# Gate and up of each feed-forward tile as a 2x2 block product of seven terms, with split weights, in a two-layer fp32 encoder

## The chip, the core and the metric

The kernel runs on one core of one Trainium2 chip. The metric is the device time of one execution in microseconds (us), the median of three runs. The matrix engine is TensorE (PE, with its weight loads apart as PEld), the elementwise engines are VectorE (DVE), ScalarE (ACT) and GpSimd (POOL), and SyncE (SP) issues the transfers.

## What is computed

Two sequences, 528 and 272 tokens with 16 learned ones in front of each, go through the same two layers. Together they are T = 800 tokens of 1024 channels. The part that the change touches is the feed-forward stage, which stands four times in the program (ffn1 and ffn2 of both layers):

```python
def swiglu(x, w_gate, w_up, w_down):
    return (jax.nn.silu(x @ w_gate) * (x @ w_up)) @ w_down
...
for layer in range(DEPTH):
    h = h + 0.5 * swiglu(rms_norm(h, norm_ffn1[layer]), ...)
    hn = rms_norm(h, norm_mix[layer])
    h = h + (even_mixer(hn, ...) if layer % 2 == 0 else fourier_mixer(hn, w_out_fourier[layer // 2]))
    h = h + 0.5 * swiglu(rms_norm(h, norm_ffn2[layer]), ...)
return rms_norm(h, norm_final)[:, N_META:]
```

Everything is float32. Gate and up are each 1024 x 2816 (D_FF), down is 2816 x 1024, so that D_FF makes 22 tiles of 128. The even layer's mixer is windowed attention beside a pooling mixer; the odd layer's is a Fourier transform over positions and channels with one output projection.

## The kernel before

**Layout.** Channels lie on the 128 partitions, so `h` is 8 tiles (KD) of 128 channels by 800 tokens. A matmul has a 128x128 block of weights as its stationary side and half of the tokens (392, 400, 400 and 384 columns in the four feed-forward stages, called f = 0 to 3 here) as its moving side. A stage that needs fewer tokens has them left out.

**Precision.** Each float32 operand is held as two fp32r parts, hi and lo. ScalarE makes hi (a copy with rounding), VectorE makes lo (the operand less hi). A product then takes three matmuls: hi by hi, hi weights by lo tokens, lo weights by hi tokens. For the weights, `split_hi` (L463) and `split_lo` (L678) do this for a whole block of 1024 or 1408 columns, out of `raw`, two slots that SyncE fills with one transfer a block (L235).

**A feed-forward stage.** `ffn` on each engine runs two halves of 11 tiles. In a half, a hardware loop takes the tiles: block 0 is the gate, block 1 the up weights of the tile, each 8 k tiles x 3 matmuls x 2 token halves = 48 matmuls, into two banks each. So a tile of D_FF takes 96 matmuls. VectorE takes the banks out times `rstd`, the reciprocal norm (L768 gate, L773 up), ScalarE takes Silu (L518), VectorE multiplies (L777), ScalarE and VectorE split the product into `act_hi` and `act_lo` (L522, L781). After the 11 tiles a second loop does down: 8 output tiles m, each 11 x 6 = 66 matmuls, and VectorE adds the result to `h` (L807, or L818 by token pieces).

**The norm.** While down of the second half runs, each finished channel tile of `h` is squared (L504), summed over tiles (L720), and, scaled by the gain, split to `xn_hi` (L495) and `xn_lo` (L709). The next stage's matmuls can begin on these before the norm is known. TensorE does `statistics` (L1048) after the first block and `broadcast` (L1058) in the middle of the second, with the power on GpSimd (L355) between them. Before f = 1 and f = 3 the split waits until the projection is done (`LATE_NORMS`).

**Order.** Each engine's instructions stand in the order written. Engines wait for one another by counting semaphores. The weights of block n+2 are split while block n's results are taken out: there are two slots, and so TensorE has at most one block in hand. In the Fourier stage, `fold` on GpSimd (L424, L425) adds and subtracts two halves of the raw block before the split, and the sine part of the result comes back by `odd` (L662) to be added to `h` by GpSimd (L447, L448) and VectorE.

The gate and up transfers are 512 KB, a block each.

## Time and profile before

| | |
|---|---|
| median of 3 runs | 2777.54 us (2775.79 to 2780.04) |
| span of the profiled execution | 2767.7 us |
| PE busy | 2682.6 us (97%) |
| PEld busy | 2602.0 us (94%) |
| DVE busy | 1025.1 us (37%) |
| ACT busy | 683.9 us (25%) |
| POOL busy | 97.2 us (4%) |
| weights and data read | 160.73 MB, 59 GB/s over the span |

The span runs from the first to the last instruction of the profiled execution. Its device time is not listed apart from the three runs; their median is 9.8 us over the span, and this difference is taken to stay. Busy PE counts a matmul until its result has landed, and matmuls overlap, so how fast TensorE goes is read from the spacing of their starts: a stretch of time over the number of matmuls in it.

### The profile page before, as it was taken

How to read it: one execution, taken by the hardware profiler on the slowest of the kernel's cores; microseconds unless marked ns; L12 is line 12 of the kernel's file. 1: busy time of each engine (PE TensorE's matmuls, PEld its weight loads, DVE VectorE, ACT ScalarE, POOL GpSimd, SP SyncE). 2: the span in 40 equal slices, each digit the busy share in tenths (PEclk: the TensorE clock that was granted, in tenths of full speed). 3: DMA queues.
4: the chain of work that ended last, by engine and by line, in shares of the span. 5: the costliest groups of instructions: out<-in, count | busy, mean ns of one | idle time of the engine just before them, and what ended most of it. 6: DMA issues, size and time to landing. Idle time of an engine off the chain costs nothing.

```text
span 2767.7 us, 35751 instructions
## 1 busy us (share of the span) xinstructions
PE 2682.6 (97%) x14700; PEld 2602.0 (94%) x14700; DVE 1025.1 (37%) x1312; ACT 683.9 (25%) x925; POOL 97.2 (4%) x101
## 2 busy tenths in 40 slices
PE   7999999999999999999999999999998799999997
PEld 7999999998359999999999999999998799999997
DVE  5332233333534333233334332233345633223333
ACT  4331122221542332112222221122233322112211
POOL 0000000004000000000000000000003300000000
PEclk9999999999889999999999999999999999999998
DMA  3122122212001121111211121112121222212221
GB/s 110 61 66 65 51 61 64 70 48 88 1 8 54 53 61 66 56 61 59 67 57 54 61 66 63 53 61 63 63 70 35 63 61 61 73 56 61 61 74 58
DMA packets 42096, 164.66 MB, mean 59 GB/s; under 512 B 4928, under 2 KB 5184, under 8 KB 41920
## 3 DMA queue, kind: packets, MB, share of 16 engines
q1 hardware_dynamic: 40464, 160.65, 18.3%
q10 hardware_dynamic: 1584, 3.38, 0.3%
q8 instruction: 29, 0.48, 0.1%
q14 instruction: 19, 0.16, 0.0%
HBM read 160.73 MB, written 3.28 MB: 59 GB/s over the span
## 4 chain that ended last, share of the span: by engine, by line
PE 74%; issue 21%; DVE 3%; ACT 1%; POOL 0%; DMA 0%; ACTq 0%; POOLq 0%; DVEq 0%; SPq 0%
PE banks L1016 68%; PE banks L1007 2%; PE banks L1136 1%; PE banks L1171 1%; PE banks L1150 1%; DVE sum_sq L720 0%; DVE w_lo L698 0%; ACT score L571 0%; PE banks L1048 0%; PE banks L1058 0%; DMA raw<-w_fourier_dram 0%; DVE h L995 0%; DVE xn_lo L709 0%; ACT square L504 0%; DVE score L902 0%
## 5 line engine op out<-in xcount | busy, mean ns | idle before, releaser
L1016 PE MATMUL banks<-xn_hi,w_hi 128*128 128x400 f32 (+2 forms) x3104 | 814.6, 343 | 26.1 <-DVE xn_lo L709 19.2
L1016 PE MATMUL banks<-xn_lo,w_hi 128*128 128x400 f32 (+2 forms) x3104 | 812.2, 343 | 0.0
L1016 PE MATMUL banks<-xn_hi,w_lo 128*128 128x400 f32 (+2 forms) x3104 | 811.5, 343 | 0.0
L463 ACT ACTIVATE w_hi<-raw 128x1024 fp32r<-128x1024 f32 (+1 forms) x258 | 294.4, 1141 | 1646.2 <-PE banks L1016 1645.9
L1016 PEld LDWEIGHTS banks<-xn_hi,w_hi 128*128 128x128 f32 x3104 | 571.5, 189 | 30.6 <-issue 23.6
L1016 PEld LDWEIGHTS banks<-xn_lo,w_hi 128*128 128x128 f32 x3104 | 572.4, 189 | 0.0
L1016 PEld LDWEIGHTS banks<-xn_hi,w_lo 128*128 128x128 f32 x3104 | 572.2, 188 | 0.0
L678 DVE TENSOR_TENSOR w_lo<-raw,w_hi 128x1024 fp32r<-128x1024 f32 (+1 forms) x258 | 344.5, 1335 | 71.0 <-ACT w_hi L463 70.6
L1016 PE MATMUL banks<-act_hi,w_lo 128*128 128x400 f32 (+2 forms) x1408 | 368.0, 342 | 0.0
L1016 PE MATMUL banks<-act_hi,w_hi 128*128 128x400 f32 (+2 forms) x1408 | 367.9, 343 | 0.0
L1016 PE MATMUL banks<-act_lo,w_hi 128*128 128x400 f32 (+2 forms) x1408 | 367.9, 342 | 0.0
L773 DVE TENSOR_TENSOR up_t<-banks,rstd 128x800 f32<-128x800 f32 (+2 forms) x88 | 86.1, 979 | 487.7 <-PE banks L1016 487.7
L1016 PEld LDWEIGHTS banks<-act_lo,w_hi 128*128 128x128 f32 x1408 | 259.0, 188 | 0.1
L1016 PEld LDWEIGHTS banks<-act_hi,w_hi 128*128 128x128 f32 x1408 | 258.9, 188 | 0.0
L1016 PEld LDWEIGHTS banks<-act_hi,w_lo 128*128 128x128 f32 x1408 | 258.6, 188 | 0.0
L768 DVE TENSOR_TENSOR gate_t<-banks,rstd 128x800 f32<-128x800 f32 (+2 forms) x88 | 86.2, 979 | 394.7 <-PE banks L1016 394.3
L818 DVE SCALAR_TENSOR_TENSOR h<-banks,h 128x256 f32<-128x256 f32 (+3 forms) x112 | 36.4, 384 | 240.9 <-PE banks L1016 240.9
L807 DVE SCALAR_TENSOR_TENSOR h<-banks,h 128x800 f32<-128x800 f32 x32 | 31.7, 992 | 246.7 <-PE banks L1016 246.7
L522 ACT ACTIVATE act_hi<-up_t 128x800 f32 (+5 forms) x88 | 76.1, 865 | 88.4 <-DVE up_t L777 88.4
L777 DVE TENSOR_TENSOR up_t<-up_t,gate_t 128x800 f32<-128x800 f32 (+2 forms) x88 | 86.3, 980 | 9.2
L781 DVE TENSOR_TENSOR act_lo<-up_t,act_hi 128x800 f32 (+5 forms) x88 | 86.2, 979 | 0.6
L518 ACT ACTIVATE gate_t<-gate_t 128x800 f32<-128x800 f32 (+2 forms) x88 | 74.7, 849 | 13.8 <-DVE gate_t L768 13.6
(131 smaller groups left out, 1206.4 us busy)
## 6 DMA issues: line engine op xcount, KB each, us to landing
raw<-gate_up_dram SPq DMA_DIRECT2D x176, 512.0 KB, 3.6
raw<-down_dram SPq DMA_DIRECT2D x64, 704.0 KB, 4.0
raw<-w_in_dram SPq DMA_DIRECT2D x10, 512.0 KB, 3.5
raw<-w_fourier_dram SPq DMA_DIRECT2D x8, 576.0 KB, 3.8
raw<-w_out_dram SPq DMA_DIRECT2D x8, 512.0 KB, 3.6
h<-x_dram ACTq DMA_DIRECT2D x8, 400.0 KB, 6.5
y_dram<-h SPq DMA_DIRECT2D x8, 400.0 KB, 2.5
raw<-tables_dram SPq DMA_DIRECT2D x4, 704.0 KB, 4.0
```

Of the source, the lines that this page charges most:

```text
L463: A.activation(w_hi[s][:, 0:k * P], raw[s][:, 0:k * P], ACT.Copy).then_inc(w_hi_done, 1)
L518: A.activation(gate_t[:, 0:W], gate_t[:, 0:W], ACT.Silu).then_inc(silu_done, 1)
L522: A.activation(act_hi[:, bass.ds(i * T, W)], up_t[:, 0:W], ACT.Copy)\
L678: V.tensor_tensor(w_lo[s][:, 0:k * P], raw[s][:, 0:k * P], as32(w_hi[s][:, 0:k * P]), ALU.subtract).then_inc(w_ready, 1)
L768: V.tensor_tensor(two(gate_t[:, 0:W]), slot(0, C), two(rstd[:, 0:W]), ALU.mult)\
L773: V.tensor_tensor(two(up_t[:, 0:W]), slot(1, C), two(rstd[:, 0:W]), ALU.mult)\
L777: V.tensor_tensor(up_t[:, 0:W], up_t[:, 0:W], gate_t[:, 0:W], ALU.mult)\
L781: V.tensor_tensor(act_lo[:, bass.ds(i * T, W)], up_t[:, 0:W], as32(act_hi[:, bass.ds(i * T, W)]), ALU.subtract)\
L807: return V.scalar_tensor_tensor(two(h[:, m, :]), slot(m % 2), 0.5, two(h[:, m, :]), ALU.mult, ALU.add)
L818: last = V.scalar_tensor_tensor(h[:, m, t:t + n], banks[:, 2 * (m % 2) + b, c:c + n], 0.5, h[:, m, t:t + n], ALU.mult, ALU.add)
L1007: ins = M.matmul(out, a, b, start=first and j == 0, stop=last and j == 2)
L1016: ins = M.matmul(banks[:, 2 * s + half, 0:cols], a, b[:, half * cols:(half + 1) * cols], start=first and j == 0, stop=last and j == 2)
```

## The change

**The tile product.** The two blocks of a tile, gate and up, are seen as the columns of a 2x2 matrix of blocks. Its inner index is the parity of the k tile (4 even, 4 odd), and the columns of the other factor are the two token halves. The eight block products become seven, in Winograd's form of Strassen's scheme. Each is 4 k tiles x 3 matmuls on one half of the tokens, 12 matmuls, and all 12 of a product go into one bank. So a tile takes 84 matmuls. Four of the seven left sides are sums of weight quarters: S1 = A21 + A22, S2 = S1 - A11, S4 = A12 - S2, S3 = A11 - A21, made by VectorE for each tile (`weight_sum`). The seven right sides, B11, T1, T2, B22, T3, B21 and N4, are made once a stage from `h` and the gain (`gained_tile`, `form_sum`, `form_high`, `form_low`).

**Sums in the banks.** P6, P7 and P4 go on accumulating in the bank of P1, and P3 in the bank of P5. Between them ScalarE copies the partial sum out (4 copies of half the tokens a tile, counted by `copied`), and VectorE adds and scales.

**Weights in units.** In place of two blocks there are 6 slots of 512 columns. A unit is one left side, or 2 or 3 k tiles of down. The tables at the head of the file give each unit's place; ScalarE is 4 units ahead of TensorE, VectorE 3, the sums 5. A transfer brings a whole tile, 1 MB.

**The rest.** Down runs in four chunks of 5, 5, 6 and 6 tiles in place of two of 11, so `h` is added to 32 times a stage, not 16; its matmuls are as many as before (8 x 22 x 6 = 1056 a stage). The forms alias buffers of the stage before, and before f = 1 and f = 3 (`late_forms`) they are split after the projection, four k tiles in one instruction. There are no hardware loops any more. In the Fourier stage the folded block is 3 units. The third part of the tables is split after the first 8 tiles of the transform.

```diff
+PRODUCTS = ("P1", "P5", "P6", "P3", "P7", "P2", "P4")
+WEIGHT_OF = ("A11", "S1", "S2", "S4", "S3", "A12", "A22")
+FORM_OF = ("B11", "T1", "T2", "B22", "T3", "B21", "N4")
+NS = 6
+SUM_AHEAD, HI_AHEAD, LO_AHEAD = 5, 4, 3
...
+        def form_sum(f, name, k):
+            C = FFN_COLS[f]
+            if name == "T1":
+                dve.wait_ge(gained, f * KD + 2 * k + 1)
+                ins = V.tensor_tensor(form(f, "T1", k), b12[:, 0:C], form(f, "B11", k), ALU.subtract)
...
+            ins.then_inc(form_added, 1)
...
+            if NORMS[i] in NORM_FFN:
+                f, k = NORM_FFN[NORMS[i]], m // 2
+                if m % 2 == 0:
+                    add_square(i, m)
+                    form_sum(f, "T1", k)
+                    form_low(f, "B11", k)
+                else:
+                    form_sum(f, "T2", k)
+                    form_sum(f, "T3", k)
+                    form_sum(f, "N4", k)
+                    dve.wait_ge(form_added, ADD_AT[f, "N4", k])
+                    form_low(f, "T1", k)
+                    add_square(i, m)
+                    for name in ("T2", "B22", "T3", "B21", "N4"):
+                        form_low(f, name, k)
...
+                for j in range(CHUNK_AT[c], CHUNK_AT[c] + n_tiles):
...
+                    if not first:
+                        up_first(j - 1, J - 1)
+                        dve.wait_ge(g1_done, J)
+                        dve.wait_ge(g2_done, J)
+                        V.tensor_tensor(gate[1 - j % 2][:, 0:W], gate[1 - j % 2][:, 0:W], rstd[:, 0:W],
+                                        ALU.mult).then_inc(scaled, 1)
+                    weights_to(n0)
+                    if not first:
+                        up_second(J - 1)
+                    weights_to(n0 + 1)
...
+                    if not first:
+                        product(j - 1, J - 1)
+                    weights_to(n0 + 2)
+                    if not first:
+                        act_low(j - 1, J - 1)
+                    weights_to(n0 + 3)
+
+                    dve.wait_ge(unit_done, n0 + 4)
+                    dve.wait_ge(copied, 4 * J + 3)
+                    V.tensor_tensor(g[:, C:W], banks[:, SUM53, 0:C], g[:, C:W], ALU.add).then_inc(g2_done, 1)
+                    weights_to(n0 + 4)
...
+                    dve.wait_ge(unit_done, n0 + 6)
+                    V.tensor_tensor(g[:, 0:C], banks[:, OWN2, 0:C], g[:, 0:C], ALU.add).then_inc(g1_done, 1)
...
+            def product(j, q):
+                n, J, name = GU[f][j] + q, f * FF_TILES + j, PRODUCTS[q]
+                pe.wait_ge(w_ready, n + 1)
...
+                elif name == "P3":
+                    bank = SUM53
+                    pe.wait_ge(copied, 4 * J + 2)
+                else:
+                    bank = j % 2
+                    pe.wait_ge(copied, 4 * J + {"P6": 1, "P7": 3, "P4": 4}[name])
...
+                for k in range(KP):
+                    if j == 0:
+                        pe.wait_ge(form_ready, LO_AT[f, FORM_OF[q], k])
+                    a_hi, a_lo = weights(n, k)
+                    b_hi, b_lo = xf_hi[:, at, k, 0:C], xf_lo[:, at, k, 0:C]
+                    M.matmul(out, a_hi, b_hi, start=fresh and k == 0, stop=False, skip_group_check=True)
+                    M.matmul(out, a_hi, b_lo, start=False, stop=False, skip_group_check=True)
+                    ins = M.matmul(out, a_lo, b_hi, start=False, stop=k == KP - 1, skip_group_check=True)
+                ins.then_inc(unit_done, 1)
```

Three places show what stands on an engine in a row. The first is VectorE in a tile in the middle of a stage. Before, the tile's loop body (gate and up out of the banks, two weight blocks, the product, its split):

```order
L768 TENSOR_TENSOR gate_t<-banks,rstd 128x784
L677 ISA
L678 TENSOR_TENSOR w_lo<-raw,w_hi 128x1024
L771 REGISTER_ALU
L773 TENSOR_TENSOR up_t<-banks,rstd 128x784
L777 TENSOR_TENSOR up_t<-up_t,gate_t 128x784
L677 REGISTER_ALU
L678 TENSOR_TENSOR w_lo<-raw,w_hi 128x1024
L781 ISA
L781 TENSOR_TENSOR act_lo<-up_t,act_hi 128x784
```

Now, the first 12 of the 19 instructions of a tile (`xf` are forms, `w_sum` the sums of weight quarters, `g` the gate, `p` the copy of P5's bank); seven more follow: three sums, three lo parts and an add to the gate:

```order
L1065 TENSOR_TENSOR up<-banks,rstd 128x392
L1095 TENSOR_TENSOR g<-g,rstd 128x784
L903 TENSOR_TENSOR w_lo<-w_sum,w_hi 128x512
L1069 TENSOR_TENSOR up<-up,p 128x392
L1071 TENSOR_TENSOR up<-up,rstd 128x392
L903 TENSOR_TENSOR w_lo<-w_sum,w_hi 128x512
L1077 TENSOR_TENSOR act<-up,g 128x784
L903 TENSOR_TENSOR w_lo<-raw,w_hi 128x512
L1083 TENSOR_TENSOR act_lo<-act,act_hi 128x784
L887 TENSOR_TENSOR w_sum<-raw 128x512
L903 TENSOR_TENSOR w_lo<-raw,w_hi 128x512
L1112 TENSOR_TENSOR g<-banks,g 128x392
```

Six elementwise instructions a tile have become 19, the two weight blocks seven units and four sums; the product of the tile before stands among the units of this one. The second place is VectorE at the program's start, one channel tile before:

```order
L709 SCALAR_TENSOR_TENSOR xn_lo<-h,gain,xn_hi 128x528
L709 SCALAR_TENSOR_TENSOR xn_lo<-h,gain,xn_hi 128x256
L720 TENSOR_TENSOR sum_sq<-sum_sq,square 128x800
L678 TENSOR_TENSOR w_lo<-raw,w_hi 128x1024
L709 SCALAR_TENSOR_TENSOR xn_lo<-h,gain,xn_hi 128x528
```

and now a pair of channel tiles, the second of the four pairs:

```order
L940 TENSOR_TENSOR sum_sq<-sum_sq,square 128x800
L956 TENSOR_TENSOR xf<-b,xf 128x392
L972 TENSOR_TENSOR xf_lo<-xf,xf_hi 128x392
L960 TENSOR_TENSOR xf<-xf 128x392
L962 TENSOR_TENSOR xf<-xf,b 128x392
L965 TENSOR_TENSOR xf<-xf 128x392
L972 TENSOR_TENSOR xf_lo<-xf,xf_hi 128x392
L940 TENSOR_TENSOR sum_sq<-sum_sq,square 128x800
L972 TENSOR_TENSOR xf_lo<-xf,xf_hi 128x392 x5
L893 TENSOR_TENSOR w_sum<-raw,w_sum 128x512
L903 TENSOR_TENSOR w_lo<-w_sum,w_hi 128x512
```

A pair takes eleven instructions of half the tokens where two tiles took four. The third place is ScalarE in the Fourier output projection, one output tile before:

```order
L662 ACTIVATE odd<-banks 128x404
L486 ACTIVATE w_hi<-w_fold 128x1024
L487 ACTIVATE w_hi<-raw 128x128
L504 ACTIVATE square<-h 128x800
L662 ACTIVATE odd<-banks 128x404
```

and now:

```order
L863 ACTIVATE odd<-banks 128x404
L566 ACTIVATE w_hi<-w_sum 128x512
L566 ACTIVATE w_hi<-raw 128x128
L566 ACTIVATE w_hi<-w_sum 128x512
L596 ACTIVATE square<-h 128x800
L615 ACTIVATE xf<-h,gain 128x384
L615 ACTIVATE xf<-h,gain 128x128
L615 ACTIVATE xf<-h,gain 128x256
L863 ACTIVATE odd<-banks 128x404
```

Three pieces of the gained tile now stand before the next `odd`, which were done after the last tile before. The hi parts here belong to output tile m+2, and GpSimd folds that block after it has added `odd` of tile m, where before it folded it ahead of that.

## Rows read from the trace of the kernel before

**Rows 1.** The page: busy us, share of the span and instructions of each engine.
```profile
PE 2682.6 (97%) x14700; PEld 2602.0 (94%) x14700; DVE 1025.1 (37%) x1312; ACT 683.9 (25%) x925; POOL 97.2 (4%) x101
```

**Rows 2.** Stretches: us, busy of PE, PEld, DVE, ACT, POOL, clock, DMA share, GB/s.
```profile
35.00:600.00 565.00, 565.00 (x3144) 564.88 (x3144) 198.33 (x229) 140.46 (x137) 0.27 (x3) 1.00 0.19 61
...
914.00:1483.00 569.00, 568.46 (x3118) 568.43 (x3119) 193.97 (x179) 141.19 (x138) 0.00 (x0) 1.00 0.19 61
...
1495.00:2050.00 555.00, 555.00 (x3055) 555.00 (x3054) 189.06 (x174) 112.89 (x115) 0.00 (x0) 1.00 0.19 63
...
2115.00:2180.00 65.00, 44.66 (x216) 42.21 (x216) 48.20 (x73) 21.82 (x34) 34.50 (x29) 0.94 0.26 79
...
2200.00:2747.00 547.00, 542.96 (x3105) 542.32 (x3103) 183.53 (x202) 107.73 (x110) 0.00 (x0) 1.00 0.19 60
```

**Rows 3.** The order in time, TensorE: start, us (L1007 puts three matmuls a step into one bank).
```profile
2073.11 0.28 PE L1007 MATMUL banks<-dft_hi,xn_lo 128*106 128x258 f32 x1
...
2074.91 0.28 PE L1007 MATMUL banks<-dft_hi,xn_lo 128*92 128x258 f32 x1
...
2173.74 0.35 PE L1007 MATMUL banks<-xn_lo,w_hi 128*128 128x404 f32 x1
...
2175.05 0.34 PE L1007 MATMUL banks<-xn_hi,w_lo 128*128 128x404 f32 x1
```

**Rows 4.** Queues in the straight-line stretch 2068 to 2115: packets, MB, share.
```profile
q8 instruction: 3, 0.05, 0.4%
```

**Rows 5.** Groups by shape: engine, operation, count | busy us, mean ns | idle before.
```profile
L678 DVE TENSOR_TENSOR w_lo<-raw,w_hi 128x1024 fp32r<-128x1024 f32 x194 | 240.7, 1241 | 56.1 <-ACT w_hi L463 55.8
...
L463 ACT ACTIVATE w_hi<-raw 128x1024 fp32r<-128x1024 f32 x194 | 205.9, 1061 | 1085.3 <-PE banks L1016 1085.0
...
L777 DVE TENSOR_TENSOR up_t<-up_t,gate_t 128x800 f32<-128x800 f32 x44 | 43.7, 993 | 4.6
...
L955 DVE TENSOR_TENSOR xn_lo<-banks,xn_hi 128x404 fp32r<-128x404 f32 x8 | 4.6, 579 | 18.6 <-ACT xn_hi L647 18.6
...
L662 ACT ACTIVATE odd<-banks 128x404 f32<-128x404 f32 x8 | 4.1, 507 | 19.1 <-PE banks L1007 19.1
```

**Rows 6.** The order in time of VectorE and ScalarE behind an up block.
```profile
1003.34 0.99 DVE L773 TENSOR_TENSOR up_t<-banks,rstd 128x800 f32<-128x800 f32 x1 [4.92 <-PE banks L1016]
...
1004.43 0.99 DVE L777 TENSOR_TENSOR up_t<-up_t,gate_t 128x800 f32<-128x800 f32 x1
...
1005.34 1.22 DVE L678 TENSOR_TENSOR w_lo<-raw,w_hi 128x1024 fp32r<-128x1024 f32 x1
...
1005.55 0.87 ACT L522 ACTIVATE act_hi<-up_t 128x800 f32 x1 [1.07 <-DVE up_t L777]
...
1006.58 0.99 DVE L781 TENSOR_TENSOR act_lo<-up_t,act_hi 128x800 f32 x1
```

**Rows 7.** The chain that ended last, around the four stage starts: start, us.
```profile
35.21 565.31 PE banks L1016 x3144
...
883.94 1.00 DVE h L931
...
890.52 11.11 PE banks L1016 x48
...
914.54 5.63 PE banks L1016 x21
...
2059.01 3.97 DMA raw<-tables_dram
...
2170.14 5.26 PE banks L1007 x27
```

**Rows 8.** GpSimd's groups in the Fourier output projection, by shape.
```profile
L425 POOL TENSOR_TENSOR w_fold<-raw 128x512 f32<-128x512 f32 x8 | 13.1, 1631 | 0.0
...
L424 POOL TENSOR_TENSOR w_fold<-raw 128x512 f32<-128x512 f32 x8 | 11.5, 1440 | 26.0 <-DMA raw<-w_fourier_dram 16.1 <-PE banks L1007 9.9
...
L447 POOL TENSOR_TENSOR h<-h,odd 128x265 f32<-128x265 f32 x8 | 8.3, 1034 | 12.0 <-ACT odd L662 12.0
```

More of the change, by code:

```diff
@@ L99, in k_tiles @@
[L99 to L111 removed]
+CHUNKS = (5, 5, 6, 6)
+CHUNK_AT = (0, 5, 10, 16)
@@ new lines, in gained_tile @@
+        def gained_tile(f, m):
+            i, k = NORMS.index(("ffn1_0", "ffn2_0", "ffn1_1", "ffn2_1")[f]), m // 2
+            if m % 2 == 0 and k:
+                act.wait_ge(form_added, ADD_AT[f, "T3", k - 1])
+            for half, c, t, n in token_parts(f):
+                if m % 2:
+                    out = xf32[:, FORM_AT["B22" if half else "B21"], k, c:c + n]
+                elif half:
+                    out = b12[:, c:c + n]
+                else:
+                    out = xf32[:, FORM_AT["B11"], k, c:c + n]
+                last = A.activation(out, h[:, m, t:t + n], ACT.Copy,
+                                    scale=gain[:, i * KD + m:i * KD + m + 1])
+            last.then_inc(gained, 1)
```

1157 lines of the change are left out of this document (708 added, 449 removed).

## The prediction

> **What bounds the kernel now.** I read the page first. TensorE is busy 2682.6 us of 2767.7, VectorE 37%, ScalarE 25% [rows 1]. A busy share does not say what a matmul costs, so the busy time by stretch comes next, for the four feed-forward stages: 565.0 us hold 3144 matmuls, 569.0 hold 3118, 555.0 hold 3055 and 547.0 hold 3105, TensorE never waits over about 4 us in any of them, and its clock is 1.00 of full, the 2.4 GHz level [rows 2]. A matmul starts every 565.0/3144 = 0.1797 us at 392 columns, 555.0/3055 = 0.1817 at 400, and 543.0/3105 = 0.1749 at 384. These stages are 2236 us of the span. The reader is to see that a matmul saved there is 0.18 us saved, as long as nothing else becomes late, and that VectorE works there only 198 of 565 us. Last I read the chain of waits at the starts of the stages, where TensorE does wait.
>
> **What is taken away.** A tile has 84 matmuls for 96: 12 x 22 = 264 fewer a stage. That is 264 x (0.1797 + 0.1817 + 0.1817 + 0.1749) = 189.6 us. Down keeps its matmuls.
>
> The Trainium skill, TensorE: Matmul & The Clock Gate, section "Wait — 56ns, not 53.3ns?", gives the spacing of back-to-back matmuls as the columns over 2.4 GHz and about 2.5 ns, so 169 ns at 400 columns. The trace disagrees: 181.7. By the page the 1056 matmuls would be worth some 176 us, by the rows 189.6.
>
> **What a matmul costs in the new form.** Twelve matmuls in a row now go into one bank; before, two banks took turns. The nearest rows are L1007, which does just this. At 258 columns 15 spacings take 1.80 us, 120 ns, 12.5 over 258/2.4; at 404 columns 7 take 1.31, 187 ns, 18.8 over 404/2.4 [rows 3]. The old form at 400 has 15.0 over. So the bounds are -2.5 and +3.8 ns, over 7392 product matmuls -18 to +28 us. Both rows are near zero on either side; I take +5 us, the side of the row nearer in columns.
>
> **VectorE in a tile.** This is where the change could fail. Times for 512 and 400 columns lie between rows: 0.579 us for 404, 0.993 for 800, 1.241 for 1024 [rows 5] give 0.575 and 0.69. A tile has 11 instructions of 512 (7 lo parts, 4 sums), 7.6 us; 5 of 400, 2.9; 3 of 800, 3.0: 13.5 us. Instructions that do not depend on the last one start 0.08 early (1004.43 + 0.99 against 1005.34 [rows 6]), which takes back about 1. TensorE needs 84 x 0.1817 = 15.3. So VectorE goes from some 35% to 80 to 90%, but it still fits. ScalarE has 7 of 512 (0.60 each, between 0.507 and 1.061 [rows 5]), 4 copies of 400 (0.51) and two of 800 (0.87 [rows 6]): 8.0 us, fits.
>
> Order can still cost. I laid a tile out, with product starts at 0, 2.2, 4.4, 6.5, 8.7, 10.9, 13.1. VectorE begins at 0.15 with the last product of the tile before, and has scaled, split units 3, 4 and 5 and made the activation by 5.8. Then it waits for the hi part of that, which ScalarE does only after its third copy: P6 ends at 6.5, copy to 7.1, hi to 8.0, lo to 9.1. The rest, 4 sums, 4 lo parts and 2 adds, is 6.6 us and ends at 15.0 to 15.7, when the next tile begins at 15.3. Unit 6 is ready at 10.4 and needed at 13.1; the copies are ready 0.6 us after a product and are needed 2.2 after, which leaves 1.6 us. The idle 2.3 us before the hi part is the buffer. TensorE does not wait: 0 us for the tile. Were VectorE's work to grow by over 15%, this cover would be gone.
>
> **Chunk ends.** Down of the last tile needs its activation: up out of the bank 0.6, product 1.0, hi 0.9, lo 1.0, with hand-overs 3.9 us by the same row as 1003.34 to 1007.57 with half as much to take out [rows 6]. TensorE meanwhile does 4 of 5 tiles of the first output, 24 x 0.18 = 4.3 us. It is covered by 0.4 us in the two short chunks of a stage, by 1.5 in the long ones. I take 1 us over eight places (0 to 4).
>
> **Starts of stages.** *f = 0:* before, TensorE had both blocks of tile 0 done at 35.2 + 24 x 0.18 = 39.5 [rows 7]. Now VectorE makes, for each pair of channel tiles, 11 instructions of 392 (0.48 each back to back), two sums of squares (0.9) and two weight steps (0.6): 8.5 us a pair, 7.6 for the first. It starts at about 10.5 and has the last forms at 43. P1 waits for its fourth k tile until 37, P5 until 39, P3 until 43, the broadcast of the norm until 48; tile 0 is done at 53.5. Without the change of order it would be 39.5 - 2.2. So +16 us (10 to 25; before, the same work was two instructions a tile). *f = 1:* last matmul of the projection at 883.9, next tile began at 914.5, 30.6 later [rows 7]. Now: h 1.0, square 0.9, sums and N4 5, B11 1.8, so P1 starts 8.5 us after, at the 1.2 GHz level for a few us (I count 10 matmuls at 0.33); forms of 1600 columns follow at 1.8 to 1.9 us and the norm's chain ends at 26; tile 1 starts at 30.0. Against 28.4: +1.5. *f = 2:* the forms are made beside down; VectorE needs about 11 to 12 us a pair beside 13.1 of TensorE, and with ScalarE's answers 13.8, so it is 1 to 2 us late at the end, and then T1 and the norm come late: +3.5 (0 to 8). *f = 3:* below.
>
> **Fourier stage.** The third part of the tables stood before the first evacuation and waited 3.97 us for its transfer [rows 7]; now it stands behind 8 tiles: -2. The first unit is 512 columns in place of 1152: -2. In the projection TensorE is busy 44.7 of 65 us [rows 2], 5.3 an output tile [rows 7]. ScalarE now has a loop: odd 0.5, GpSimd's two adds 1.8, the fold of the block two ahead 1.4 + 1.6 [rows 8], the hi part 0.6, the square 0.9, the gained pieces 1.3, which is 8.3 against some 7.7 now; +5 over eight. Then the late forms: the next tile starts some 2 us later than the old order would give. Together +7 (0 to 15).
>
> **The sum.** -189.6 + 5 + 0 + 1 + 16 + 1.5 + 3.5 - 2 - 2 + 7 = -159.6 us. From the profiled span of 2767.7 this is 2608. The 9.8 us between span and median stay: 2777.5 - 160 = **2618 us**.
>
> **Instruction stream.** The loops are gone, and TensorE's matmuls and weight loads all stand in line. The stretch 2068 to 2115 stands in line too, at 366 matmuls in 47 us, with three fetches [rows 4] and no wait for them; it goes faster than the products will. So 0. The Trainium skill, Runtime: NRT & Kernel Launch, section "Instruction fetch mechanics", says that a taken branch out of the window stalls and straight code streams. By it the loops would have cost something and dropping them gain; the trace shows no such stall in the loops [rows 2], and the sum would be the same.
>
> **The rivals.** *VectorE becomes the bound of the tile* (0.12). For it: 13.5 us of 15.3 and five hand-overs between VectorE and ScalarE in each tile. Against: the 2.3 us buffer. If its instructions and hand-overs come to 16.1 us a tile, TensorE waits 0.8 a tile: 88 x 0.8 = 70, 2688 us. *One bank, many waits* (0.08): each product has one or two waits of its own, and twelve matmuls into one bank cost 3.8 ns more each, 28 us in place of 5; with 20 ns at each of 616 units, 12 us more: 2653. *The forms hide* (0.05): the starts cost 5 and not 28: 2595. *Slower than before* (0.03): ScalarE's copy between P1 and P6, P5 and P3, P6 and P7, P7 and P4 is the place. It has 1.6 us of slack each. If ScalarE is held up there by the weight sums it waits for, so that each of the four copies comes 2.1 us late, 0.5 us are lost four times a tile: 176 us, over the 160 gained; 2794. It decides from a lateness of 2.05 us a copy on. *It doesn't do what it says:* the order of the built program has 7392 product matmuls; none. A chance of 0.01 lies in a gain eaten to zero by two of these at once.
>
> **How the numbers follow.** The forecast, TensorE undisturbed in the tiles, has 0.71: 2618, from 2600 to 2650 by the bounds above. The range takes in the second and third rival and part of the first: 2594 to 2665. A change under 0.2% (5.6 us) can't be told from none. Faster: 0.71 + 0.12 + 0.08 + 0.05 = 0.96; same 0.01; slower 0.03.
>
> **What would show it.** 13644 matmuls, 1056 fewer than [rows 1]. In a stretch of tiles: spacing 0.180 to 0.186 us at 400 columns, VectorE busy 80 to 90%, TensorE without waits over 0.3 us. Tile 0 of the first stage done near 53 us. The projection of the Fourier stage 67 to 72 us. If TensorE waits inside tiles for `w_lo` of VectorE, the laid-out tile is wrong; if it waits for a copy, ScalarE's order is; if the spacing is over 0.19 without waits, it is the bank.

## The result

| | before | after |
|---|---|---|
| median, us (lowest to highest, runs) | 2776.66 (2771.79 to 2780.04, 4) | 2607.76 (2607.15 to 2614.92, 4) |
| profiled execution: span, us | 2767.7 | 2605.3 |
| matmuls | 14700 | 13644 |

The ratio is 0.9406, with a 95% interval from 0.9388 to 0.9424: 169 us faster. The prediction had 2618, from 2594 to 2665. A second set of five executions of the same kernel, on the chip of experiments e8, e9 and e11, had a median of 2608.96 (2606.87 to 2610.30), ratio 0.940.

The page of after, beside [rows 1]; then the queue that brings the instructions:

```profile
PE 2496.2 (96%) x13644; PEld 2415.1 (93%) x13644; DVE 1657.6 (64%) x2900; ACT 1046.5 (40%) x2015; POOL 90.9 (3%) x101
...
q8 instruction: 110, 1.80, 0.3%
```

TensorE has 186 us less of busy time; VectorE has 633 us more and still a third of the span to spare. The straight code asks for 110 instruction packets, and TensorE has no wait for them inside a tile.

The four stretches of tiles, with the columns of [rows 2]: us, then busy time and instructions of PE, PEld, DVE, ACT, POOL.

```profile
58.00:560.00 502.00, 502.00 (x2818) 502.00 (x2817) 335.17 (x607) 200.87 (x358) 0.00 (x0) 1.00 0.20 68
881.00:1393.00 512.00, 512.00 (x2817) 512.00 (x2817) 339.76 (x541) 209.65 (x382) 0.00 (x0) 1.00 0.19 66
1420.00:1932.00 512.00, 512.00 (x2817) 512.00 (x2817) 329.58 (x512) 199.15 (x354) 0.00 (x0) 1.00 0.19 65
2087.00:2582.00 495.00, 495.00 (x2820) 495.00 (x2819) 321.04 (x566) 190.31 (x346) 0.00 (x0) 1.00 0.19 64
```

TensorE is busy for the whole of all four. A matmul starts every 502/2818 = 0.1781 us at 392 columns, 0.1818 at 400 and 0.1755 at 384. [rows 2] had 0.1797, 0.1817 and 0.1749. So twelve in a row into one bank cost nothing, within 2 ns either way. Differences of this size are not the bank's alone: in experiment e2 below, whose matmuls are the same, the pace was 174.4 ns in place of 176.1 at 384 columns, and the four stretches took 2017.1 us for 2022.8. Why is open.

One tile of after, 15.3 us, first as a stretch and then as VectorE's and ScalarE's order in time (start, us):

```profile
1003.60:1018.90 15.30, 15.30 (x86) 15.30 (x85) 12.10 (x20) 7.51 (x13) 0.00 (x0) 1.00 0.20 70
```
```profile
1003.41 0.57 DVE L1069 TENSOR_TENSOR up<-up,p 128x400 f32<-128x400 f32 x1
...
1005.11 0.98 DVE L1077 TENSOR_TENSOR act<-up,g 128x800 f32<-128x800 f32 x1
1006.01 0.69 DVE L903 TENSOR_TENSOR w_lo<-raw,w_hi 128x512 fp32r<-128x512 f32 x1
1009.28 0.99 DVE L1083 TENSOR_TENSOR act_lo<-act,act_hi 128x800 fp32r<-128x800 f32 x1 [2.58 <-ACT act_hi L698]
...
1007.98 0.50 ACT L695 ACTIVATE g<-banks 128x400 f32<-128x400 f32 x1 [1.17 <-PE banks L1440]
1008.38 0.86 ACT L698 ACTIVATE act_hi<-act 128x800 fp32r<-128x800 f32 x1
```

The tile goes as it was laid out by hand. VectorE is busy 12.1 of 15.3 us, 79%. Its one long wait, 2.58 us where the prediction had 2.3, is for the hi part of the activation, which ScalarE makes only after the copy at 1007.98.

**Where 162 us of span went.** I compared the start times of the same matmuls in both traces: the first of a stage, the first of its tile 1, the last of down (and of w_out, the output projection of the attention mixer). The prediction's terms are put on the same cuts. A start there has lost the 12 matmuls of tile 0, 2.1 to 2.2 us, which stand against its cost.

| piece of the span | before, us | after, us | difference | predicted |
|---|---|---|---|---|
| f = 0: start to tile 1 | 39.37 | 57.90 | +18.5 | +13.8 |
| tile 1 to the last matmul, four stages | 2207.4 | 2022.8 | -184.7 | -175.2 |
| f = 0's last to w_out's last (attention inside) | 292.09 | 287.75 | -4.3 | 0 |
| w_out's last to tile 1 of f = 1 | 30.98 | 33.04 | +2.1 | -0.7 |
| f = 1's last to tile 1 of f = 2 | 20.38 | 26.64 | +6.3 | +1.3 |
| f = 2's last to tile 1 of f = 3 (Fourier stage) | 153.97 | 154.27 | +0.3 | +0.9 |
| the end | 23.44 | 22.97 | -0.5 | 0 |
| sum | | | -162.3 | -159.9 |

Whether the 4.3 us of the third row belong to the change is open. The experiments, whose code is the same there, took from 287.6 to 296.5 us for it, which is more than the difference, and of the kernel before there is one trace.

### The profile page after: what moved, and what is told of

It is laid out like the page before. It is cut to its first block, busy times and chain, and to the rows that moved or that the text cites. A ratio compares the mean times of both kernels' runs of the same rounds, so it can differ in the third digit from the quotient of the medians.

```text
span 2605.3 us, 35440 instructions
## 1 busy us (share of the span) xinstructions
PE 2496.2 (96%) x13644; PEld 2415.1 (93%) x13644; DVE 1657.6 (64%) x2900; ACT 1046.5 (40%) x2015; POOL 90.9 (3%) x101
## 4 chain that ended last, share of the span: by engine, by line
PE 71%; issue 22%; DVE 4%; ACT 2%; POOL 1%; DMA 0%; POOLq 0%; ACTq 0%; DVEq 0%
PE banks L1361 26%; PE banks L1438 13%; PE banks L1440 13%; PE banks L1439 13%; PE banks L1491 2%; PE banks L1526 1%; PE banks L1505 1%; PE banks L1354 1%; DVE xf_lo L972 1%; ACT xf L615 0%; DVE xf_lo L985 0%; POOL w_sum L516 0%; POOL w_sum L518 0%; PE banks L1400 0%; ACT xf_hi L626 0%
## 5 line engine op out<-in xcount | busy, mean ns | idle before, releaser
L1438 PE MATMUL banks<-xf_hi,w_hi 128*128 128x400 f32 (+2 forms) x2464 | 848.7, 344 | 70.3 <-DVE xf_lo L985 23.4
L1439 PE MATMUL banks<-xf_lo,w_hi 128*128 128x400 f32 (+2 forms) x2464 | 848.7, 344 | 0.0
L1440 PE MATMUL banks<-xf_hi,w_lo 128*128 128x400 f32 (+2 forms) x2464 | 846.1, 343 | 0.0
L1438 PEld LDWEIGHTS banks<-xf_hi,w_hi 128*128 128x128 f32 x2464 | 466.3, 189 | 73.6 <-issue 51.7
L1440 PEld LDWEIGHTS banks<-xf_hi,w_lo 128*128 128x128 f32 x2464 | 468.5, 190 | 0.0
L1439 PEld LDWEIGHTS banks<-xf_lo,w_hi 128*128 128x128 f32 x2464 | 466.7, 189 | 0.4
L566 ACT ACTIVATE w_hi<-raw 128x512 fp32r<-128x512 f32 (+3 forms) x564 | 310.4, 559 | 373.5 <-PE banks L1361 365.6
L566 ACT ACTIVATE w_hi<-w_sum 128x512 fp32r<-128x512 f32 x368 | 230.3, 630 | 332.7 <-DVE w_sum L895 128.6
L903 DVE TENSOR_TENSOR w_lo<-raw,w_hi 128x512 fp32r<-128x512 f32 (+3 forms) x564 | 337.0, 611 | 19.3 <-ACT w_hi L566 19.3
L903 DVE TENSOR_TENSOR w_lo<-w_sum,w_hi 128x512 fp32r<-128x512 f32 x368 | 252.4, 689 | 2.6 <-ACT w_hi L566 2.6
L679 ACT ACTIVATE g<-banks 128x400 f32<-128x400 f32 (+2 forms) x88 | 43.9, 499 | 217.5 <-PE banks L1440 217.5
```

What stands on the lines that cost most here:

```text
L566: A.activation(w_hi[:, n % NS, 0:u.cols], source, ACT.Copy).then_inc(w_hi_done, 1)
L903: V.tensor_tensor(w_lo[:, n % NS, 0:u.cols], source, as32(w_hi[:, n % NS, 0:u.cols]), ALU.subtract).then_inc(w_ready, 1)
L1438: M.matmul(out, a_hi, b_hi, start=fresh and k == 0, stop=False, skip_group_check=True)
L1439: M.matmul(out, a_hi, b_lo, start=False, stop=False, skip_group_check=True)
L1440: ins = M.matmul(out, a_lo, b_hi, start=False, stop=k == KP - 1, skip_group_check=True)
```

## The experiments

Line numbers in the rows of an experiment are those of its own kernel. Unless another is named, times are set against 2607.8 us, the changed kernel.

**Is it the number of matmuls?** P2 is done twice:

```diff
-                for k in range(KP):
+                for k in [*range(KP), *range(KP)] if name == "P2" else range(KP):
```

> The twelve matmuls of P2 are done twice in each tile (the second start of the bank throws the first twelve away), so a tile has 96 matmuls again, as before the change, but in the new form: same output, 14700 matmuls. Theory (the number of matmuls sets the time of the tiles, everything else is covered): 264 more a stage at the spacings of the changed kernel, 0.178 + 0.182 + 0.182 + 0.176 us, is +189 us, so 2797 us, some 20 us over the kernel before, which is then what the starts of the stages cost. Rival A (part of the gain comes from something else, the code without loops or a faster pace in one bank): then the 96 matmuls cost clearly less than +189, and the time is at or under the 2777 of the kernel before. Rival B (VectorE or ScalarE already holds TensorE back a little in each tile): a longer tile gives that time back, so again less than +189, by the part that was waiting.

Measured: 2798.57 us (2797.09 to 2804.51), ratio to before 1.0098, interval 1.0073 to 1.0122. That is 190.8 more than the changed kernel, where 189 was expected. Both kinds of rival fall: at most a few us of the gain can belong to the straight code, and no engine was holding TensorE back in the tiles. With the same 14700 matmuls the new form is 28 us slower than the old one on the same chip (2770.35). By the cuts of the table, the starts of the stages cost 35 us in this run, the tiles and down 3.6 less than before (2203.9 for 2207.4), and the third row 4.1 less. So the price lies at the starts, not in the tiles.

**How much cover has VectorE?** Four additional instructions, eight in the second kernel, each waiting for the last (the wait and its semaphore are left out here), stand ahead of the lo part of the activation:

```diff
                     weights_to(n0 + 2)
+                    if j:
+                        for _ in range(4):
+                            V.tensor_tensor(fill[:, :], rstd[:, 0:400], rstd[:, 360:760], ALU.add)
                     if not first:
                         act_low(j - 1, J - 1)
```

> The changed kernel with four extra VectorE instructions of 400 columns in tiles 1 to 21 of each stage, each waiting for the last one (some 0.60 us each, 2.4 us in all), put just ahead of the lo part of the activation, where VectorE waits 2.6 us for ScalarE. Theory (cover of 2.3 to 2.6 us at that place): no change, within 0.2%: 2608 +- 5. Rival (VectorE is in fact the bound of the tile, or its steps are so tight that any delay passes through): 84 x 2.4 = +202 us, 2810; in between, whatever part of the 2.4 passes through times 84.

> The same with eight extra VectorE instructions, 4.8 us a tile. VectorE is idle 3.2 us in a tile of 15.3, so 1.6 us a tile are too much. Theory (cover of 3.2 us a tile, then VectorE is the bound): each chunk of five or six tiles falls behind by 1.6 a tile, of which some 2.7 us are taken by the weights that lie ready (unit 6 is ready at 10.4 and needed at 13.1) and VectorE catches up in down: 84 x 1.6 = 134 less 16 x 2.7 = 43, so +90 us, 2700 (from 2650 to 2745). Rival (much more cover than the order laid out by hand says, because TensorE is fed far ahead): under +30 us. Rival (VectorE the bound from the first addition on): +400 us.

Measured: 2603.12 us (2601.51 to 2604.26) with four, 2690.96 (2686.99 to 2694.51) with eight. Two stretches of the first, and what TensorE waited for in the second (us in total, times, longest):

```profile
881.00:1393.00 512.00, 512.00 (x2822) 511.88 (x2821) 386.52 (x626) 210.33 (x383) 0.00 (x0) 1.00 0.19 66
...
1000.00:1060.00 60.00, 60.00 (x332) 59.98 (x331) 55.18 (x89) 28.38 (x51) 0.00 (x0) 1.00 0.14 50
```
```profile
PE banks L1446 <- ACT up L711: 51.6, 42, 1.6
...
PE banks L1369 <- DVE act_lo L1085: 10.8, 16, 1.2
```

VectorE can be busy 55.18 of 60 us, 92%, and TensorE does not notice (that the kernel is 4.6 us faster than without the four is the pace spoken of above, and not explained). So the first 2.4 us a tile are free, and the rival that VectorE is nearly the bound falls. With 4.8 us the cover of 3.2 us a tile is used up: +83 us where +90 was expected. The wait that then ends last is of interest. It is not one for VectorE's weights but for ScalarE's copy `up`, 42 times. ScalarE goes through its list in order, and the hi part of a weight sum stands ahead of that copy; when VectorE is late with the sum, ScalarE waits for it and the copy comes late. One such place, ScalarE and then TensorE:

```profile
209.59 0.63 ACT L568 ACTIVATE w_hi<-w_sum 128x512 fp32r<-128x512 f32 x1 [4.77 <-DVE w_sum L889]
210.13 0.48 ACT L711 ACTIVATE up<-banks 128x392 f32<-128x392 f32 x1
...
210.75 0.42 PE L1446 MATMUL banks<-xf_hi,w_hi 128*128 128x392 f32 x1 [1.30 <-ACT up L711]
```

That is the mechanism of the prediction's slower rival. It exists, and it begins somewhere between 2.4 and 4.8 us of VectorE work a tile away from the kernel as it is.

**How late may a copy be?** `late(j, p)` is so many ScalarE instructions of 608 columns, 0.71 us each, behind the wait for the product and ahead of copy p: four at copy 4 in the first kernel, one at each of the four copies in the other.

```diff
+                    late(j, 4)
                     A.activation(up[:, C:W], banks[:, acc, 0:C], ACT.Copy).then_inc(copied, 1)
```

> The changed kernel with four extra ScalarE instructions of 608 columns (about 0.70 us each, 2.8 us in all) in tiles 1 to 21 of each stage, behind the wait for P7 and ahead of the copy that frees P7's bank for P4. The copy is ready 0.5 us after P7 ends and P4 begins 2.2 after, so the prediction has 1.65 us of slack there. Theory: 2.8 - 1.65 = 1.15 us of wait a tile at P4, 84 x 1.15 = +97 us, 2705; the hi parts behind it come 2.8 later too and may add up to 0.5 a tile: 2690 to 2750. Rival (another wait hides it, the copies have more slack than 1.65 us): under +40 us. Rival (late hi parts pass fully through VectorE to the weights): 84 x 2.8 = +235 us.

> One extra ScalarE instruction of 608 columns (0.71 us) ahead of each of the four copies out of the banks in tiles 1 to 21, so that every copy is 0.7 us late. The run with 2.85 us at the last copy alone lost 1.57 a tile, so the slack there is 1.3 us. Theory (each copy has its own 1.3 us and a lateness under it costs nothing): the tiles as they were, span 2605 +- 5. Rival (the four add up along the chain through VectorE, whose idle time outside the wait for the hi part is only 0.6 us a tile): up to 84 x 0.8 = +67 us.

Measured: 2742.81 us (2742.08 to 2751.26), +135, for the four at one copy. What TensorE waited for, and one tile:

```profile
PE banks L1450 <- ACT up L721: 113.9, 84, 1.4
```
```profile
1050.29:1067.16 16.87, 15.54 (x86) 15.23 (x85) 12.19 (x20) 10.03 (x17) 0.00 (x0) 1.00 0.18 63
```

There are 84 waits, one a tile, and no others inside tiles: the mechanism is as expected, but the price was to be 97. A tile takes 16.87 us for 15.30, so 1.57 are lost by 2.85 of lateness: the slack is 1.3 us, not 1.65. In the changed kernel's trace the copy is ready 0.70 us after the next product starts and is needed at 2.19, where the prediction had 0.6 and 2.2, and here the waiting matmul starts 0.14 us after the copy's end. That leaves 1.35. The profile counts the wait (1.36) from the last result, 0.34 after that matmul's start, where the next one otherwise starts after 0.18; with this 0.16 it is 1.52 of the 1.57 that the tile loses.

With 0.71 us at each of the four copies the tiles and down of the four stages took what they had (501.6, 512.4, 511.5 and 497.6 us, 2023.1 in sum, for 2022.8). So the four slacks don't add up into one. The span was 2611.5; what it has over 2605.3 lies in the attention stage, where no instruction was added.

**Can GpSimd take work from VectorE at the starts?** `add_square` is made by GpSimd for f = 0 and f = 2:

```diff
+        def add_squares(i):
+            for m in range(1, KD):
+                pool.wait_ge(sq_done, i * KD + m + 1)
+                if m > 1:
+                    pool.wait_ge(sum_done, 7 * i + m - 1)
+                nc.gpsimd.tensor_tensor(sum_sq[:, :], sum_sq[:, :], square[:, :], ALU.add)\
+                    .then_inc(sum_done, 1)
```

> The sums of squares of the norms ahead of f = 0 and f = 2 (seven additions of 800 columns each) are made by GpSimd in place of VectorE; nothing else changes. Theory (VectorE's work for each pair of channel tiles sets the start of f = 0, 8.4 us a pair, and makes f = 2 begin late): 1.8 us less a pair. f = 0: tile 1 starts at 57.9 - 3.5 x 1.8 = 51.6 us. f = 2: VectorE has its last addition to h some 3 us earlier, and from f = 2's first matmul to tile 1 it takes 23.5 us in place of 26.5. Together -9 us. Rival (GpSimd and VectorE hold each other up: GpSimd's additions of 831 columns took 1.64 us, an addition of VectorE of 1024 columns 1.24 alone and more beside GpSimd): VectorE's instructions beside an addition of GpSimd grow by as much as was saved, and both starts stay within 1 us; if GpSimd holds the whole time, 2 x 1.6 in place of 1.8 a pair, f = 0 starts 5 us later.

Measured: one execution, 2617.18 us, span 2615.4. Tile 1 of f = 0 starts at 62.0 us, 4.1 later; P1's last k tile starts at 43.9 us for 39.5, and a pair takes 9.6 to 9.8 us for 8.4. From f = 2's first matmul to tile 1 it takes 31.5 us in place of 26.5. The theory fell and the rival holds, in its worst form. GpSimd's addition, and VectorE beside it:

```profile
25.10 2.24 POOL L469 TENSOR_TENSOR sum_sq<-sum_sq,square 128x800 f32<-128x800 f32 x1 [3.99 <-ACT square L607]
```
```profile
25.05 0.56 DVE L976 TENSOR_TENSOR xf<-xf 128x392 f32<-128x392 f32 x1
25.64 2.13 DVE L983 TENSOR_TENSOR xf_lo<-xf,xf_hi 128x392 fp32r<-128x392 f32 x1
```

The instruction that began before GpSimd's kept its 0.56 us. The next one took 2.13 in place of 0.56 and ended 0.4 us after GpSimd's did. So it goes for all 14 additions: beside each, one VectorE instruction ends 0.42 to 0.44 us after GpSimd's, whenever it began. By that it stands still rather than going slower. Eleven of the 14 took 1.6 to 1.7 us longer than alone, the other three, which began a good 1 us into GpSimd's, some 0.8. Moving the addition saved VectorE 0.9.

**What sets the start of f = 2?** The sum and the two lo parts between the last two additions to h go behind the last one, with their hi parts on ScalarE:

```diff
-                    weights_to(n + 1, limit)
+                    if not (final and f == 1 and m == KD - 1):
+                        weights_to(n + 1, limit)
...
                     form_low(f, "T1", k)
+                    if next_unit is not None:
+                        next_unit += 1
+                        weights_to(next_unit)
                     add_square(i, m)
```

> In the last down chunk of f = 1, the weight steps that stood between the addition of the seventh output tile to h and that of the eighth (one sum, two lo parts on VectorE, their hi parts on ScalarE) move behind the last addition, in between the forms. Theory (f = 2 begins late since VectorE reaches the last addition to h 4.4 us after TensorE is through with it): that addition comes 1.8 us sooner, at 2.6 in place of 4.4 after the last down matmul, and from f = 2's first matmul to tile 1 it takes some 24.5 us in place of 26.5: -2 us, all else as it was. Rival (the weights are then late: P6 and P3 wait for them in place of the forms): the same 26.5 or more.

VectorE at the end of f = 1 in the changed kernel; the last down matmul starts at 1393.75:

```profile
1392.65 0.98 DVE L1048 SCALAR_TENSOR_TENSOR h<-banks,h 128x800 f32<-128x800 f32 x1
1394.58 0.99 DVE L940 TENSOR_TENSOR sum_sq<-sum_sq,square 128x800 f32<-128x800 f32 x1 [0.94 <-ACT square L596]
...
1398.49 0.98 DVE L1048 SCALAR_TENSOR_TENSOR h<-banks,h 128x800 f32<-128x800 f32 x1
...
1402.26 0.57 DVE L972 TENSOR_TENSOR xf_lo<-xf,xf_hi 128x400 fp32r<-128x400 f32 x1
```

TensorE's waits there in the changed kernel, and then in the experiment:

```profile
PE banks L1438 <- DVE xf_lo L972: 4.7, 2, 3.6
```
```profile
PE banks L1446 <- DVE xf_lo L976: 2.9, 2, 1.8
PE banks L1398 <- DVE sum_sq L944: 1.3, 1, 1.3
```

Measured: 26.0 us from f = 2's first matmul to tile 1, for 26.5. The wait for the forms fell by 1.8, just the time that was moved, and 1.3 came back as a wait for the sum of squares, ahead of which a weight step now stood (a sum and a lo part, 1.2 us). The last addition came 2.6 us after the last down matmul, as expected, and still only 0.4 of the 2 us were left. Even these are not shown: executions with the unaltered code there took from 26.5 to 27.3 us, and e11 and e12, which have the edit, 26.8. (The one execution had 2611.28 us; tile 1 of f = 0 began 3.7 us later in it, with the same code. The last section comes to that.)

**What sets the starts of f = 1 and f = 3?** B11 by k tile, and its lo parts ahead of the form N4:

```diff
+            for k in range(KP):
+                form_low(f, "B11", k)
             V.tensor_tensor(xf32[:, FORM_AT["N4"], :, 0:C], xf32[:, FORM_AT["B21"], :, 0:C],
                             xf32[:, FORM_AT["T2"], :, 0:C], ALU.subtract).then_inc(form_added, 1)
```

> At the starts of f = 1 and f = 3, where P1 waits 8.3 us for one hi and one lo instruction of 1600 columns, the form B11 is made by k tile (four of 400 each), its lo parts ahead of the form N4. Theory (the start is set by how soon P1 can begin and by the chain behind it): P1 begins some 2.5 us sooner in both; T1's lo part then comes as late as before, since VectorE has the same work, so tile 1 starts 1 to 2 us sooner in each: -3 us together. Rival (the chain of the norm and VectorE's 1600-column forms set the end of tile 0, and P1's begin does not matter): tile 1 starts at the same time, 33.0 us after the last projection matmul in f = 1 and 25.0 after P1 in f = 3.

TensorE's waits at the start of f = 1, in the changed kernel and then here:

```profile
PE banks L1438 <- DVE xf_lo L985: 8.0, 1, 8.0
PE banks L1438 <- issue: 3.4, 1, 3.4
```
```profile
PE banks L1447 <- DVE xf_lo L976: 4.9, 1, 4.9
PE banks L1447 <- issue: 2.1, 1, 2.1
PE banks L1447 <- DVE xf_lo L994: 1.1, 1, 1.1
```

Measured: one execution, 2600.22 us, span 2598.4 for 2605.3. w_out's last matmul to tile 1 of f = 1 takes 31.2 us for 33.0; f = 2's last to tile 1 of f = 3 148.6 for 154.3. Of these 5.7, 3.7 lie behind the projection's last matmul (37.1 for 40.8); the 2.0 ahead of it come and go with the same code (e8 has them too). The theory holds, with some more gained at f = 3. P1 begins 3.1 us sooner at f = 1 and tile 1 only 1.8. The waits behind P1 are no longer than they were (3.2 us for 3.4). What comes back is the clock: 25 matmuls of the products start 0.33 us apart for 16, at 0.15 us each 1.3 us.

**What sets the start of f = 0?** TensorE sums the squares of the first norm in the statistics bank, a round of eight small matmuls for each square, and VectorE adds none; the squares go to two buffers in turn:

```diff
+        def first_statistics(m):
+            pe.wait_ge(sq_done, m + 1)
...
+            for k in range(KD):
+                ins = M.matmul(banks[0:100, STAT, k:k + 1],
+                               (square if m % 2 else sum_sq)[:, 100 * k:100 * k + 100], ones[:, 0:1],
+                               start=m == 0, stop=m == KD - 1, skip_group_check=True)
+            ins.then_inc(sum_done if m < KD - 1 else stat_done, 1)
```

> At the start of f = 0 alone, TensorE sums the squares: the eight statistics matmuls of a channel tile follow each square (accumulated in the bank over the eight tiles, 56 more small matmuls than before, while TensorE waits for the forms anyway), and VectorE's seven additions of 800 columns are gone. Theory (VectorE, busy all the time there, sets the 8.4 us a pair): 1.8 us less a pair, but ScalarE is busy 22.0 of 25 us there, so it takes over as the bound at some 7.4 us a pair: tile 1 starts at 57.9 - 3.5 x 1.0 = 54.4, and 1 us more as the statistics don't stand behind P5: 53.5. Rival (the pace of a pair is the chain of hand-overs between ScalarE and VectorE, not VectorE's work): no change of the pace, 57.

> The changed kernel again, unaltered, for comparison with the next one on the same chip: 2608 +- 4 us, ratio 0.940 to the kernel before. Both theories expect the same; it shows by how much its starts vary from one execution to the next (runs so far had tile 1 of f = 0 start at 57.7 to 61.6 us with the same code).

> The three edits of the starts together: the first form by k tile (f = 1, 3), the last addition to h ahead of the weight steps (f = 2), and the statistics as the squares come (f = 0). Theory (the starts are independent of one another and of the tiles, so the gains add): -5.5 (measured for the first: 1.8 at f = 1, 3.7 at f = 3) - 0.4 - 4 = -10 us against the changed kernel on the same chip, ratio 0.9365 to the kernel before. Rival (TensorE's clock, lost in the waits at a start, is given back later and eats part): -5 us or less.

> The three edits of the starts, with two things altered at f = 0: the first two rounds of statistics stand ahead of TensorE's wait for the first weights (in e9 and e11 ScalarE waited 5.0 us there for its square's buffer), each odd round stands behind P1's matmuls of its pair; and the eight columns of the statistics bank are set to zero first by VectorE and only accumulated into, with no start mark. Theory (in e9 the pace of a pair was 7.54 us with ScalarE always busy, and only the first round's wait spoiled it): P1's last k tile starts near 36 us in place of 39.5, P5 near 39.3 in place of 40.3, statistics no longer stand behind it, so tile 1 starts at 55.3 us in place of 57.8; with what e11 showed elsewhere (its w_out to tile 1 of f = 1 31.2 in place of 33.0 us, f = 2's end to tile 1 of f = 3 147.1 in place of 154.2) the time is 2599 +- 4 us, ratio 0.9365. Rival (TensorE's clock eats the gain: more cold matmuls after an earlier begin, and the same total): tile 1 at 57 or later, 2603 or more.

The times of e9 and e11 are those of the full work, but their first norm lacks the squares of channels 0 to 127 for tokens 0 to 699; why is in the last section. e12 computes all of it.

| kernel | median, us (range, runs) | ratio to before | f = 0: tile 1 starts, us |
|---|---|---|---|
| e9, statistics edit alone | 2612.78 (1) | | 62.5 |
| e10, changed kernel again | 2608.96 (2606.87 to 2610.30, 5) | 0.9400 (0.9383 to 0.9418) | 57.8 |
| e11, three edits | 2605.99 (2605.72 to 2611.05, 5) | 0.9390 (0.9372 to 0.9407) | 61.8 |
| e12, three edits, mended | 2601.33 (2599.45 to 2608.25, 5) | 0.9390 (0.9373 to 0.9407) | 56.0 |

The start of f = 0: a stretch of the changed kernel, a stretch and two rows of ScalarE's order in time of e9, and a stretch of e12:

```profile
23.00:39.50 16.50, 2.44 (x7) 1.40 (x7) 16.43 (x31) 14.98 (x33) 0.00 (x0) 1.00 0.00 1
```
```profile
23.00:45.00 22.00, 20.97 (x116) 20.67 (x116) 17.74 (x35) 21.90 (x48) 0.00 (x0) 1.00 0.01 1
```
```profile
22.73 0.87 ACT L596 ACTIVATE sum_sq<-h 128x800 f32<-128x800 f32 x1 [4.99 <-PE banks L1399]
...
30.29 0.85 ACT L596 ACTIVATE sum_sq<-h 128x800 f32<-128x800 f32 x1
```
```profile
20.00:40.00 20.00, 19.85 (x106) 19.16 (x106) 17.63 (x35) 19.94 (x44) 0.00 (x0) 1.00 0.01 2
```

In the changed kernel VectorE is busy 16.43 of 16.50 us: it sets the pace of 8.4 us a pair. Freed of the sums it is busy 17.74 of 22, and ScalarE 21.90 of 22: the pace is 7.5 us a pair (22.73 to 30.29) and ScalarE is the bound, as expected. e9 lost it again at one place that I had not seen: the first round stood behind TensorE's wait for the first weights, and ScalarE waited 4.99 us for the buffer. With that mended tile 1 starts at 56.0, where 55.3 was expected, 1.8 us sooner than in e10.

Against e10, on the same chip, e11 is 3.0 us faster where 10 were expected, which is the rival's figure but not its reason. In the profiled execution f = 0 took 4.0 more by the place just named, and the third row of the table 7.6 more. e12's 2601.3 us lie in its 2599 +- 4, its ratio of 0.9390 misses the 0.9365.

e12 against e10: f = 0 -1.8 us, f = 1 -1.7, f = 2 +0.4, Fourier stage with the start of f = 3 -7.1. The medians differ by 7.6 us, 0.3%, but e12 ran on another chip, on which the kernel before was also 4.4 us faster (2770.71 for 2775.15); the ratios differ by 0.1%. By the medians e12 is the fastest kernel here of those that ran more than once, but its range overlaps that of e10 and so do the intervals of the ratios, so a gain in the whole time is not shown. What is shown are the shorter starts of f = 1 and f = 3, which recur in e7, e11 and e12. The traces say why it stays unclear: the attention stage, which no edit touches, took 134.6 us in the profiled execution of e12 and 128.3 in that of e10. The two stretches, e12 and then e10:

```profile
648.30:782.90 134.60, 126.91 (x403) 52.84 (x401) 67.38 (x271) 68.56 (x262) 0.00 (x0) 0.80 0.02 9
```
```profile
650.10:778.40 128.30, 121.36 (x402) 51.41 (x400) 67.20 (x271) 68.57 (x262) 0.00 (x0) 0.83 0.03 9
```

The work is the same and the granted clock is not: 0.80 and 0.83.

## Right or wrong, step by step

- **The matmuls taken away, right.** Doing them again costs 190.8 us; the prediction had 189.6 for them. The Trainium skill, TensorE: Matmul & The Clock Gate, section "Wait — 56ns, not 53.3ns?", would by its spacing have had an estimated 176. By e1 the rows are right and that spacing is not, for this kernel.
- **The pace in one bank, on the wrong side.** +5 was taken, from bounds of -18 to +28. The stretches of tiles gained 9.5 us more than predicted, 8.5 of it pace (0.1782 us for 0.1797 at 392 columns) and 1 the chunk ends, which cost nothing. The row that I held to be nearest (404 columns, 18.8 ns over) was from another stage, with seven spacings, and did not carry over.
- **VectorE in a tile, right.** 12.1 us of 15.3 for a predicted 12.5, a wait of 2.58 for 2.3. (79% busy is just under the 80 to 90% named as a sign.) The cover was put at "over 15%" more work, 2 us; it is 3.2 us a tile by the trace, and 2.4 more cost nothing.
- **The slack of a copy, right in kind and too large:** 1.3 us for 1.6; the prediction left out the hand-over behind the copy (0.14 us) and took the copy as ready 0.1 too soon. With that, the slower rival would have decided from 1.75 us of lateness (160/352 and the slack).
- **Starts of stages, the terms that were mis-sized.** The three that stand alone cost 20.7, 4.2 and 8.4 us (the table's differences and the 2.2 that tile 0 lost), 33 together, where 16, 1.5 and 3.5 were predicted, 21. At f = 0 the pace was right, 8.4 us a pair for 8.5. But P1's last k tile came at 39.5 and not at 37 (VectorE's first form waits for ScalarE's gained pieces until 12.4, where 10.5 was taken for the start), and P5 then ran at the 1.2 GHz level: a matmul of 392 columns every 0.327 us, twelve of them, 1.8 us. At f = 1 I counted 10 matmuls at that level. There are 16, each 0.15 us dearer, and with the first ones behind the two waits it is 3.1 us for the 1.5 priced. At f = 2 I had VectorE 1 to 2 us late; it is 4.4 us late at the last addition to h (1398.49 against 1394.1, when the last down matmul is through), and TensorE waits 1.1 and 3.6 us and then has 9 matmuls at the lower level, 2.1 us with the first ones behind the waits. So one step failed all three times: the clock after a wait was left out or priced too low, by 1.8, 1.6 and 2.1 us. At f = 0 and f = 2 the wait itself was too small as well, by 2.5 us and by 2.4 to 3.4 us of VectorE's lateness. Of f = 1's excess some 1 us stays open.
- **Fourier stage, right in sum by two errors.** Predicted +0.9, measured +0.3. The projection was to slow down by 5 us (to 67 to 72, from a cut of 65); it took 53.5 us from its first matmul to its last, for 57.5. Up to there the stage takes 8.3 less than before, and the start of f = 3 then 8.6 more (40.8 us from the projection's last matmul to tile 1, for 32.2). The loop that I had laid out is there after the change: `odd` follows ScalarE's gained pieces without a wait, GpSimd waits for `odd`, ScalarE for the fold. But from the third output tile on a turn takes 7.0 to 7.6 us and not 8.3. The two folds take 2.6 us; the 1.4 + 1.6 were means of the kernel before, where single ones took up to 2.3. And before, an output tile took up to 9.1 us, with GpSimd's fold waiting for its weights; that wait is gone. One turn after the change, then GpSimd's waits in the projection, before and after:

```profile
2007.01 0.48 ACT L863 ACTIVATE odd<-banks 128x404 f32<-128x404 f32 x1
...
2007.57 0.75 POOL L540 TENSOR_TENSOR h<-h,odd 128x265 f32<-128x265 f32 x1 [3.09 <-ACT odd L863]
...
2010.44 0.63 ACT L566 ACTIVATE w_hi<-w_sum 128x512 fp32r<-128x512 f32 x1 [2.95 <-POOL w_sum L516]
...
2014.16 0.49 ACT L863 ACTIVATE odd<-banks 128x404 f32<-128x404 f32 x1
```

```profile
POOL w_fold L424 <- DMA raw<-w_fourier_dram: 16.1, 5, 5.0
POOL h L447 <- ACT odd L662: 6.7, 4, 4.5
```
```profile
POOL h L540 <- ACT odd L863: 35.1, 7, 16.6
```

- **From span to median, wrong by 8 us,** the largest part of the 10 between 2618 and 2607.8. "The 9.8 us between span and median stay" took a spread between executions for something fixed. The profiled execution of after took 2607.15 us for a span of 2605.3, so 1.85 us lie outside the span; by that the profiled execution of before took some 2769.6, at the quick end of what the kernel before has in all these runs (2767.57 to 2780.66). Against the span itself, 2608, the measured 2605.3 is 2.7 off. That closeness is in part luck: the starts that stand alone cost 12 us more than predicted, and the tiles 9.5 less and the third row 4.3 less took it back.
- **The rivals:** VectorE is no bound (e2), the bank has no price, the forms do not hide (33 us at three starts), and the copies are in time. The forecast's range of 2600 to 2650 held the result; one result can't tell whether 0.71 was the right chance.

## What to carry to other kernels

Where one engine is busy all the time, lay out one period of the loop by hand with the other engines' queues in it. It gave the free time of VectorE to 0.4 us and the wait that holds it to 0.3, and the price of eight added instructions to 10%. The price of a late copy it gave less well (97 us for 135), since 0.3 us of slack too many count 84 times. Added work on the engine that looks near its limit is a cheap test: the share of busy time does not tell (92% was free, in the right place). Price the start of a stage apart, with the lower clock after each wait, and look for the engine with no idle time there; take work from it only towards an engine that does not stop it.

## What the hardware did that I had not expected

- **GpSimd stops VectorE.** A fp32 addition of two SBUF operands on GpSimd, 2.24 us, held a VectorE instruction that began inside it from 0.56 to 2.13 us, and one was held so beside each of the 14 additions of e5. One that had begun before it kept its 0.56, as did one that began 0.01 us into it.
- **The start mark of a bank is not the column's own.** In e9 and e11 each of the eight columns of the statistics got its own start mark in the first round, and seven more rounds were added. The sums of tokens 0 to 699, the first seven columns, lack the squares of the first round. The relative error of the two outputs, 0.10847 and 0.0853, is that of the reference computed with just these squares left out (0.10847 and 0.0853; with those of tokens 0 to 599 left out the second would be 0.051, with those of all 800 it would be 0.109). In e12 the bank is set to zero first and no start mark is given, and nothing is missing. The reading that fits: a start in one column makes the next matmul into the other columns of the bank overwrite what is there, so that only the last column started keeps its first round. No run tests the mark by itself. In the kernel before, where each column is started and finished before the next, nothing is lost.
- **The clock after a wait differs between executions.** With the same code at f = 0, TensorE did 109 matmuls between 40 and 60 us in one execution and 88 in another, both busy all the time (the changed kernel, then e6). In the first, 13 of the products' matmuls start 0.33 us apart, the 1.2 GHz level at 392 columns, in the second 29:

```profile
40.00:60.00 20.00, 20.00 (x109) 19.66 (x108) 16.39 (x28) 8.74 (x18) 1.94 (x1) 1.00 0.15 53
```
```profile
40.00:60.00 20.00, 20.00 (x88) 19.62 (x87) 13.15 (x23) 8.00 (x17) 1.94 (x1) 1.00 0.15 53
```

  That is 3.7 us of the start, and it does not show in the clock column (1.00 in both); the count of matmuls shows it. A difference of 4 us in one execution says nothing on an edit, unless the piece of the trace it belongs to is compared, as with P1's last k tile in e5 (43.9 us; in e6 it is at 39.5 like in the changed kernel).
